# Decoder stack on one core: the first attention's value projections moved ahead of its heads, with tokens on the partitions

## What is computed

```python
h = rms_norm(x, norm_w[1])
proj = h @ w_in                       # q, k, v, z of 1024 columns each, and one forget gate per head
c = cumsum(log_sigmoid(f + b_f))      # per head, over the tokens
s = q @ k.T / sqrt(128) + c_i - c_j   # causal
o = softmax(s) @ v
y = (o * silu(z)) @ w_out
x = x + y
```

## Time and profile before

| | |
|---|---|
| median of 3 runs | 2057.83 us (2055.85 to 2057.93) |
| profiled execution, its own time | 2058.19 us |
| its span in the profile | 2056.4 us |
| granted TensorE clock, mean | 0.997 |
| TensorE busy | 2026.1 us, 99% |
| VectorE busy | 1460.5 us, 71% |
| ScalarE busy | 554.1 us, 27% |
| GpSimd busy | 351.3 us, 17% |

### The profile page before, as it was taken

How to read it: one execution, slowest core, us unless ns; L and a number is a source line. 1 busy time by engine, 2 the same in 40 slices (tenths; PEclk the granted TensorE clock), 3 DMA queues, 4 the chain that set the end, 5 groups by cost and what they waited for, 6 DMA issues and landing times.

```text
span 2056.4 us, 31827 instructions
## 1 busy us (share of the span) xinstructions
PE 2026.1 (99%) x12942; PEld 1626.2 (79%) x12942; DVE 1460.5 (71%) x2281; ACT 554.1 (27%) x970; POOL 351.3 (17%) x320
## 2 busy tenths in 40 slices
PE   8999999999999999999999999999999999999999
PEld 6888788887777777777778877777888888888887
DVE  5766666667777777667888887576656778949973
ACT  2000122222545444323663234444310010000000
POOL 2212111111101110011111211111112122212221
PEclk9999999999999999999999999999999999999999
DMA  4323222222211122122112332111223332322332
GB/s 161 113 92 103 83 90 86 93 83 75 83 62 55 63 68 65 57 72 82 62 62 73 123 101 87 62 46 48 77 82 100 101 103 93 102 93 93 103 98 87
DMA packets 53361, 173.80 MB, mean 85 GB/s; under 512 B 6336, under 2 KB 6720, under 8 KB 53088
## 3 DMA queue, kind: packets, MB, share of 16 engines
q1 hardware_dynamic: 48112, 161.74, 24.1%
q10 hardware_dynamic: 5104, 10.03, 1.7%
HBM read 169.58 MB, written 2.16 MB: 84 GB/s over the span
## 4 chain that ended last, share of the span: by engine, by line
PE 48%; DVE 5%; ACT 1%; issue 0%; DVEq 0%; ACTq 0%
PE ps_lin L1818 14%; PE ps_lin L1820 13%; PE ps_lin L1819 13%; PE ps_att L1864 4%; PE ps_aux L1864 2%; DVE arena L415 1%; ACT arena L1275 1%; DVE w_lo L415 1%; PE ps_att L1873 0%; DVE arena L901 0%; DVE arena L421 0%; DVE y_lo L415 0%; DVE sq L415 0%; DVE xw_lo L421 0%; DVE x L415 0%
## 5 line engine op out<-in xcount | busy, mean ns | idle before, releaser
L1818 PE MATMUL ps_lin<-xw_hi,w_hi 128*128 128x512 f32 (+1 forms) x1728 | 699.1, 405 | 1.5 <-DVE w_lo L415 1.5
L1820 PE MATMUL ps_lin<-xw_hi,w_lo 128*128 128x512 f32 (+1 forms) x1728 | 675.3, 391 | 0.0
L1819 PE MATMUL ps_lin<-xw_lo,w_hi 128*128 128x512 f32 (+1 forms) x1728 | 674.1, 390 | 0.0
L397 POOL TENSOR_SCALAR w_hi<-raw 128x1024 fp32r<-128x1024 f32 (+5 forms) x312 | 347.4, 1114 | 1689.9 <-PE ps_lin L1820 1562.5
L415 DVE TENSOR_TENSOR w_lo<-raw,w_hi 128x1024 fp32r<-128x1024 f32 (+2 forms) x344 | 378.8, 1104 | 48.3 <-POOL w_hi L397 18.0
L1275 ACT ACTIVATE arena<-arena 128x512 f32<-128x512 f32 (+7 forms) x331 | 206.4, 631 | 751.4 <-DVE arena L415 362.9
L1820 PEld LDWEIGHTS ps_lin<-xw_hi,w_lo 128*128 128x128 f32 (+1 forms) x1728 | 322.7, 187 | 71.6
L1818 PEld LDWEIGHTS ps_lin<-xw_hi,w_hi 128*128 128x128 f32 (+1 forms) x1728 | 323.1, 187 | 70.0 <-issue 3.7
L1819 PEld LDWEIGHTS ps_lin<-xw_lo,w_hi 128*128 128x128 f32 (+1 forms) x1728 | 323.5, 187 | 60.8
L415 DVE TENSOR_TENSOR arena<-ps_lin,rstd 128x512 f32<-128x512 f32 (+2 forms) x213 | 146.7, 689 | 201.3 <-PE ps_lin L1820 186.8
L1818 PE MATMUL ps_lin<-y_hi,w_hi 128*128 128x512 f32 (+1 forms) x544 | 205.4, 378 | 1.3 <-DVE w_lo L415 1.1
(11 more groups left out here) (176 smaller groups left out, 1702.9 us busy)
## 6 DMA issues: line engine op xcount, KB each, us to landing
raw<-in_w_up SPq DMA_DIRECT2D x44, 512.0 KB, 3.3
raw<-in_conv_w_in SPq DMA_DIRECT2D x32, 512.0 KB, 3.3
raw<-in_fox_w_in SPq DMA_DIRECT2D x32, 512.0 KB, 3.3
raw<-in_gdn_w_in SPq DMA_DIRECT2D x32, 512.0 KB, 3.3
raw<-in_w_gate SPq DMA_DIRECT2D x24, 512.0 KB, 3.3
raw<-in_swa_w_in SPq DMA_DIRECT2D x20, 512.0 KB, 3.2
raw<-in_w_ml SPq DMA_DIRECT2D x16, 512.0 KB, 3.5
raw<-in_w_down SPq DMA_DIRECT2D x16, 512.0 KB, 3.6
```

Of the source, the lines that this page charges most:

```text
L397: pool.tensor_scalar(w_whole(n, kc * c)[0], w_raw(n, kc * c), 1.0, 0.0, mult, add).then_inc(s("w_rounded"), 1)
L1818: pe.matmul(o, wh, hi, start=first and k == 0, stop=False)
L1819: pe.matmul(o, wh, lo, start=False, stop=False)
L1820: ins = pe.matmul(o, wl, hi, start=False, stop=last and k == kc - 1)
```

## The change

The weight stream begins the layer with eight units of v weights, four chunk pairs for each of two groups of four heads (512 columns). `fox_values` multiplies them with blocks of `xw` as the loaded operand: 128 tokens by 512 channels for each of four token blocks, in the four banks of `ps_att`. ScalarE copies each bank into `vt0` or `vt1` and scales by `rc`, which holds `rstd` as a column; to have it, TensorE turns four blocks of `rstd` into `ps_aux` after the second unit and VectorE copies them. A head is left with the tiles q, k, z. The turn of v, its evacuation and its copy go. The value product of head h and what VectorE does with it (`fox_out`) stand one round later, after tile q and ahead of the scores of the next head.

```diff
@@ stream
+    for g in range(2):
+        tiles[("fox_w_v", g)] = len(tiles)
+        for k in range(0, ND, 2):
+            units.append(("fox_w_v", g, k, 2, T, "xw1", T, k == 0, k == ND - 2, len(tiles) - 1))
     for h in range(FOX_H):
-        for part in range(4):
+        for part in (0, 1, 3):
             tile("fox_w_in", part * FOX_H + h, ND, P, "xw1")
@@ vector, after fox_c
+            dve.wait_ge(s("rows_turned"), 1)
+            dve.tensor_copy(F["rc"], ps_aux[:, 0:NT * 8].rearrange("p (a b) -> p a b", a=NT)[:, :, 0]).then_inc(s("columns"), 1)
+            dve.wait_ge(s("columns"), made("columns"))
+            weights(tile_of("fox_w_v", 0))
+            weights(tile_of("fox_w_v", 1))
+            def fox_out(h):
+                dve.wait_ge(s("sm_out"), h + 1)
+                dve.wait_ge(s("z_silu"), h + 9)
+                tt(v_tmp[:], ps_aux[:], F["z"][:, h % 2, :], mult).then_inc(s("head_out"), 1)
+                dve.wait_ge(s("head_out"), made("head_out"))
+                split(v_tmp[:], y_hi[:, h, :], y_lo[:, h, :], "y_ready")
             for r in range(FOX_H + 1):
...
                 if r == FOX_H:
                     weights(tile_of("fox_w_out", 0))
+                if r > 1:
+                    fox_out(r - 2)
...
                 if r < FOX_H:
-                    evac(tile_of("fox_w_in", 16 + r), F["v"][:, r % 2, :])
+                    evac(tile_of("fox_w_in", 24 + r), F["z"][:, r % 2, :])
...
-                if r < FOX_H:
-                    evac(tile_of("fox_w_in", 24 + r), F["z"][:, r % 2, :])
-                if h >= 0:
-                    dve.wait_ge(s("sm_out"), h + 1)
...
+            fox_out(FOX_H - 1)
@@ scalar
+            act.wait_ge(s("columns"), 1)
+            for g in range(2):
+                t = tile_of("fox_w_v", g)
+                for i in range(NT):
+                    if i < NT - 1:
+                        act.wait_ge(s("v_turned"), (NT - 1) * g + i + 1)
+                        activation(F["vt"][g][:, i, :], ps_att[:, i, :], ACT.Copy, scale=F["rc"][:, i:i + 1]).then_inc(s("v_out"), 1)
...
-                    act.wait_ge(s("v_turned"), h + 1)
-                    activation(F["vt"].rearrange("p a b -> p (a b)"), ps_aux[:], ACT.Copy).then_inc(s("v_out"), 1)
@@ tensor
+            def fox_values(units):
+                for _ in range(units):
+                    n, k0, g = at[0], UNITS[at[0]][2], UNITS[at[0]][1]
+                    need("w_split", n + 1)
+                    for kk in range(2):
+                        k, part = k0 + kk, slice(kk * T, (kk + 1) * T)
+                        for i in range(NT):
+                            if g and k == 0:
+                                if i < NT - 1:
+                                    pe.wait_ge(s("v_out"), i + 1)
...
+                            hi, lo = blk(xw_hi[:, k, :], i), blk(xw_lo[:, k, :], i)
+                            pe.matmul(ps_att[:, i, :], hi, w_hi[:, n % SPLIT, part], start=k == 0, stop=False)
+                            pe.matmul(ps_att[:, i, :], hi, w_lo[:, n % SPLIT, part], start=False, stop=False)
+                            last = pe.matmul(ps_att[:, i, :], lo, w_hi[:, n % SPLIT, part], start=False, stop=k == ND - 1)
...
+            def fox_pv(h):
+                pe.wait_ge(*aux("head_out", h + 1))
+                for j in range(NT):
+                    pe.wait_ge(s("fox_pt_act" if j % 2 else "fox_pt_dve"), 2 * h + j // 2 + 1)
+                    last = mm(ps_aux[:, j * P:], blk(F["vt"][h // 4][:, j, :], h % 4), F["PT"][:, j, j * P:], j == 0, j == NT - 1)
...
+            fox_values(2)
+            pe.wait_ge(s("rstd_ready"), 2)
+            pe.wait_ge(*aux("columns", 1))
+            for i in range(NT):
+                last = tr(ps_aux[:, i * 8:(i + 1) * 8], blk(rstd[0:8, :], i), n=8)
...
+            fox_values(6)
             tile()
             for r in range(FOX_H + 1):
...
                 if 0 < r < FOX_H:
                     tile()
+                if r == FOX_H:
+                    three(0, 1)
+                if r > 1:
+                    fox_pv(r - 2)
...
                 if r < FOX_H:
-                    tile()
+                    tile(2)
                 else:
-                    three(0, 1)
...
-                        last = tr(blk(ps_aux, i), blk(F["v"][:, b, :], i))
...
-                    three(1, 4)
+                    three(1, 5)
...
-            three(5, ND)
+            three(5, 6)
+            fox_pv(FOX_H - 1)
+            three(6, ND)
```

More of the change, by code:

```diff
@@ L257, in block_program @@
         A = carve()
-        fox = dict(q=A(2, T), k=A(2, T), v=A(2, T), z=A(2, T), L=A(NT, T), PT=A(NT, T), cb=A(T), vt=A(NT, P),
-                   c=A(T), ab=A(T), r1=A(T), ones=A(T), st=A(3, NT))
+        fox = dict(q=A(2, T), k=A(2, T), z=A(2, T), vt0=A(NT, T), L=A(NT, T), PT=A(NT, T), cb=A(T), vt1=A(NT, T), st=A(3, NT), rc=A(NT))
+        fox.update(c=fox["vt1"][:, 0, :], ab=fox["vt1"][:, 1, :], r1=fox["vt1"][:, 2, :], ones=fox["vt1"][:, 3, :], vt=[fox["vt0"], fox["vt1"]])
         A = carve()
@@ L429, in subtract @@
                 if ASIDE.get(n) == "fox_w_out":
-                    dve.wait_ge(s("v_turned"), FOX_H - 1)
+                    dve.wait_ge(s("sm_out"), FOX_H // 2)
                 elif ASIDE.get(n) == "swa_w_out":
@@ L1364, in _ @@
             fox_row(0)
+            act.wait_ge(s("columns"), 1)
[5 more added lines that the diff above has]
+                        activation(F["vt"][g][:, i, :], ps_att[:, i, :], ACT.Copy, scale=F["rc"][:, i:i + 1]).then_inc(s("v_out"), 1)
+                        act.wait_ge(s("v_out"), made("v_out"))
+                    else:
+                        act.wait_ge(s("unit_done"), LAST_UNIT[t] + 1)
+                        activation(F["vt"][g][:, i, :], ps_att[:, i, :], ACT.Copy, scale=F["rc"][:, i:i + 1]).then_inc(bank_read(t), 1)
             for r in range(FOX_H + 1):
@@ L1920, in _ @@
                     tile()
+                if r == FOX_H:
+                    three(0, 1)
+                if r > 1:
+                    fox_pv(r - 2)
+                if h == 0:
+                    pe.wait_ge(s("v_out"), FOX_V)
+                    for g in range(2):
+                        pe.wait_ge(bank_read(tile_of("fox_w_v", g)), reads(tile_of("fox_w_v", g)))
                 if h >= 0:
@@ L1950, in _ @@
                                 last.then_inc(s("sm_turned"), 1)
[L1951 to L1957, removed]
-                        pe.wait_ge(s("fox_pt_act" if j % 2 else "fox_pt_dve"), 2 * h + j // 2 + 1)
-                        last = mm(ps_aux[:, j * P:], F["vt"][:, j, :], F["PT"][:, j, j * P:], j == 0, j == NT - 1)
-                        if j == NT - 1:
-                            last.then_inc(s("sm_out"), 1)
-            three(5, ND)
+            three(5, 6)
+            fox_pv(FOX_H - 1)
+            three(6, ND)
             tile(ND - BANKS)
@@ L1972, in gdn_columns @@
                 pe.wait_ge(s("rows_ready"), 2)
-                pe.wait_ge(*aux("columns", 1))
+                pe.wait_ge(*aux("columns", 2))
                 for i, name in enumerate(("beta", "be", "el", "r2")):
@@ L2235, in _ @@
             pe.wait_ge(s("rows_ready"), 3)
-            pe.wait_ge(*aux("columns", 2))
+            pe.wait_ge(*aux("columns", 3))
             for j in range(NT):
```

29 lines of the change are left out of this document (18 added, 11 removed).

## The result

The changed kernel takes 2061.49 us in the median of 12 runs (2057.99 to 2062.81), the kernel before 2057.83 us (2055.85 to 2059.97): a ratio of 1.0016, 95% interval 1.0009 to 1.0024. The profiled execution took 2061.41 us, near the median; its span is 2059.6 us, 3.2 more than before's 2056.4.

A forecast was written before the change was run, and what follows sets the result against it. The prediction took TensorE, busy throughout the first attention, to bound the kernel. Its terms, -4.1 + 2.6 + 0.3 + 1.3 = +0.1 us, laid on the median of 2057.83, gave 2058.0 us, range 2054.8 to 2062.

The forecast's parts named there:

- What leaves TensorE: First attention: the turn of the values goes, value products cost as before; gain 4.1 us.
- The start: Values' stage: TensorE waits for transposes of rstd, copy and subtraction in sequence; loss 2.6 us, bounds 2.0 and 2.9.
- The collision that I added from the earlier trace: Values' stage: GpSimd's rounding and VectorE's subtraction exclude each other; raises the loss there from 2.0 to 2.6 us.
- The round: Each head: period 21.81 us, probabilities ready at 15.1 to 15.5 against 15.5; loss 0.3 us in all, bounds 0 and 3.5.
- rival 3: Head rounds become bound by the softmax, each growing by the probabilities' lateness; 2065 us, or 2061.7 for half; chance 0.14.
- The last round: Output projection's first chunk waits 1.8 us for a subtraction; with 0.65 back and 0.15 lost, loss 1.3 us, bounds 0.9 and 1.7.
- The clock: TensorE's granted clock may fall at the new pause at the start, as near 540, where it costs 1.7 us.
- no change of clock: The forecast itself: pauses as summed, TensorE's clock unchanged, 2058.0 us; chance 0.48.
- a fall at one of the new pauses: Rival: TensorE's clock falls at one of the new pauses, 1.7 us more, 2059.7; chance 0.22.
- Sum +0.1: Whole change: -4.1 + 2.6 + 0.3 + 1.3 us, without change of clock.
- no change within 0.2%: Whole kernel: time stays within 4.1 us of the kernel before; chance 0.83, slower 0.12, faster 0.05.
- The pause near 540: TensorE's existing wait after sixteen small transposes; a rival had its clock no longer fall, 2056.3 us, chance 0.08.

The follow-up runs named there:

- The longer chain: Changed kernel with one additional VectorE instruction of 128x512 at the end of each head's output, its result not used: 2062.99 us, ratio 1.0025 to the kernel before.
- the early turn: Changed kernel with the four transposes of rstd after the first value unit instead of the second: 2057.81 us, ratio 1.0000 to the kernel before.
- the first pause filled: Changed kernel with eight additional matmuls, results not read, between the transposes of rstd and the third value unit: 2058.21 us, ratio 1.0000 to the kernel before.
- the subtraction first: Changed kernel with VectorE's subtraction of the third value unit ahead of its wait for the transposes of rstd: 2058.40 us, ratio 1.0004 to the kernel before.
- the last round split: Changed kernel with the first output projection chunk's third tile behind head 7's scores, and VectorE copying head 6's turned probabilities before evacuating head 7's z: 2056.73 us.
- the chunk moved: Changed kernel with the last round's first output projection chunk moved whole behind head 6's value product and head 7's scores: 2058.23 us, ratio 1.0001 to the kernel before.

## Why the prediction was right, and where not

**What leaves TensorE: right.** A value unit is as fast as a tile (its matmuls follow each other in 0.23 us at full clock), the round went from 27.77 to 21.80 us (forecast 21.81), and 3.75 us of work left TensorE (forecast 3.8, with the new transposes).

**The start: right.** The third unit begins at 255.47 where the second ends at 252.99 (its last matmul begins at 252.76, and they follow each other in 0.23 us), a loss of 2.48 us (forecast 2.6). All of it lies some 0.3 us earlier than forecast, since the layer begins 0.38 us earlier in this profile. The collision that I added from the earlier trace rows came. Seen by itself, the first of the three subtractions is

```profile
253.31 1.05 POOL L402 TENSOR_SCALAR w_hi<-raw 128x1024 fp32r<-128x1024 f32 x1 [4.38 <-PE ps_att L1954]
253.79 1.63 DVE L420 TENSOR_TENSOR w_lo<-raw,w_hi 128x1024 fp32r<-128x1024 f32 x1
```

It takes 1.63 us where 1.22 is usual, and ends at 255.42, 1.06 us after the rounding. In the round it is the same: the subtraction at 385.27 ends at 386.93, 1.07 us after the rounding beside it. I had put 0.65 us for it and it cost 0.41. The Trainium skill describes the exclusive lock ("SBUF — State Buffer", Who interferes with whom); the trace agrees nearly: had the subtraction stood still until the rounding's end, it would have ended 1.22 us after it, and it ended some 0.15 us sooner, both times.

**The round: right.** The last probability is ready 15.32 us after the value product, inside my 15.1 to 15.5, and no round has an idle time. The longer chain puts the moment at which it is wanted at 15.62 - 0.17 = 15.45 (forecast 15.5). So the round was within 0.15 us of the edge from which, by rival 3, each round grows.

**The last round: right.** Wait 1.79 us (forecast 1.8). That the same chunk hides the copies I did not see; it needed the run that moved it.

**The clock: here the forecast failed.** The step is the choice of "no change of clock" as the likeliest case, with 0.48, and 0.22 for a fall at one of the new pauses. The clock fell at both, in both profiles of the changed kernel, and that is 3.12 us; two falls at once were no case of the list. My argument against it was the window near 960 of the earlier trace rows, idle for 1.58 us at full clock, and that the pause in the last round has nothing small ahead; neither kept the clock up. The page of the Trainium skill on the clock gate ("TensorE: Matmul & The Clock Gate", Loop structure matters more than you think) spoke for 1.7 us and was nearer, though its own case is a long DMA wait between every matmul and not one pause of 2 us. Sum +0.1, two falls 3.1: 3.2 us, and that is the difference of the spans.

The runs themselves agree: time and mean granted clock of all 12 of the changed kernel,

```
2057.99 0.998    2061.41 0.996    2061.72 0.995
2058.75 0.997    2061.48 0.996    2061.95 0.995
2060.63 0.996    2061.51 0.996    2062.05 0.995
2060.99 0.996    2062.32 0.995    2062.81 0.995
```

The two runs whose clock is as high as before's profile (0.997) or higher took 2058 to 2059 us, the forecast. A mean doesn't say where the clock was low: near 880 us it is low in both kernels too (878 to 883: 0.50 before, 0.69 after), outside what the change touches.

**The range held by luck.** The forecast was 2058.0 us, 0.2 over the kernel before, and the measured median is 3.7 over it. The upper end of 2062 stood for the better half of rival 3, late rounds at 2061.7, and no round was late; what filled the room were two falls of the clock. That the change would count as no change within 0.2% came true with 3.7 of 4.1 us.

## What to carry to other kernels

Where one engine is full, an instruction taken from it is worth its length, but count next what its new order waits for: here 4.2 us were won and as much lost again at two places where a subtraction stood one position too late in another engine's queue. A wait that comes from queue order costs nothing to mend (the transposes one unit earlier, or the subtraction ahead of the wait); a piece of work that looks like the cause of a wait may at the same time hide another, so split it before moving it. A longer chain on one engine need not come out longer by what was added: 0.43 of 0.73 us went into a collision that no longer took place, so read the length of each row before you call the rest slack. And a pause of some two microseconds between dense matmuls cost about 1.5 us more here each time that the clock fell behind it, which was not each time.

## What the runs showed that I had not expected

The fall of the clock is neither sure nor tied to the pause alone. With the same wait of 1.79 or 1.80 us in the last round the window was at low clock in the changed kernel (both profiles) and in the one with the early turn, and at 1.00 in the ones with the first pause filled and with the subtraction first. In the one with the longer chain the waits there are 0.37 and 2.08 us, more than in any of these, and the clock from 455 to 470 is 1.00. At the start the wait of 1.99 us is there in the profile with the last round split too, and its window from 255 to 260 is at 1.00, where the changed kernel (both profiles), the one with the chunk moved and the one with the longer chain are at 0.66. Where a pause was taken away or filled, no profile shows a fall at its place. The pause near 540 kept its clock in the profiles with the chunk moved as a whole, the subtraction first, and the last round split, and lost it in the others. So two profiles can differ by some 1.5 us for each such pause. That the pause is what the falls need is shown at the start of the attention, by filling it; for the last round it is likely and not shown, since the fall there also stayed away with its pause in place. What decides it was not settled, and I did not try to.
